# The scan's output and the gate rows ahead of the out projection: half of the output worked out inside the scan, gates broadcast by DMA

## The reference

```python
mu = jnp.mean(y, axis=-1, keepdims=True)
var = jnp.mean(jnp.square(y - mu), axis=-1, keepdims=True)
yn = ((y - mu) * lax.rsqrt(var + GN_EPS)).reshape(bn, s, A_WIDTH) * prm['gn_w'] + prm['gn_b']
bonus = jnp.sum(f['r'][:, :, None] * f['k'] * prm['r_k'], axis=(2, 4))
yn = yn + (bonus[..., None] * f['v']).reshape(bn, s, A_WIDTH)
return (yn * f['g']).astype(dtype)
...
return out_lat, jnp.concatenate([a_ctx, b_ctx], axis=-1) @ w_out
...
h_lat = h_lat + ml[2] * rms_norm_2(o_lat, g_post_mix[i])
```

## Time and profile before

| | |
|---|---|
| median of 3 runs | 2166.06 us |
| lowest, highest | 2158.6, 2166.61 us |
| the profiled execution | 2172.52 us |
| its span | 2169.9 us |
| granted clock, mean | 0.946 |
| busy share: PE, DVE, ACT, GpSimd | 91%, 53%, 41%, 12% |

### The profile page before, as it was taken

One profiled execution on the slowest core, in us unless ns is written; L12 is line 12 of the kernel. 1 busy time (PEld: TensorE's weight loads), 2 busy tenths in 40 slices (PEclk: granted clock), 3 DMA queues, 4 the chain that ended last, 5 costly groups with the idle time before them and its releaser, 6 DMA issues. The chain is left out here.

```text
span 2169.9 us, 36714 instructions
## 1 busy us (share of the span) xinstructions
PE 1977.5 (91%) x15607; PEld 1634.5 (75%) x15607; DVE 1142.5 (53%) x1799; ACT 880.5 (41%) x1560; POOL 257.0 (12%) x292
## 2 busy tenths in 40 slices
PE   5997999898899999997899968989999979888998
PEld 4746998675799788664788837878888768667986
DVE  4555675555577554346655574354444545435643
ACT  4354654445366443353322233232222344545542
POOL 1100221110022100003211071020000021002000
PEclk9987999998899999997899989999999989998999
...
GB/s 245 175 284 104 182 188 185 146 195 290 99 192 179 172 118 86 131 180 12 6 4 3 4 78 78 97 79 97 97 97 97 79 39 135 21 20 131 181 187 122
DMA packets 230936, 261.34 MB, mean 120 GB/s; under 512 B 14070, under 2 KB 153590, under 8 KB 230647
## 3 DMA queue, kind: packets, MB, share of 16 engines
...
q10 hardware_dynamic: 9424, 2.95, 0.7%
...
## 5 line engine op out<-in xcount | busy, mean ns | idle before, releaser
L399 PE MATMUL acc<-rounded,rounded 128*128 128x512 f32 (+1 forms) x2552 | 881.9, 346 | 35.7 <-DVE rounded L643 11.2
L400 PE MATMUL acc<-rounded,rounded 128*128 128x512 f32 (+1 forms) x2552 | 876.9, 344 | 0.0
L401 PE MATMUL acc<-rounded,rounded 128*128 128x512 f32 (+1 forms) x2552 | 875.9, 343 | 0.0
L383 DVE TENSOR_TENSOR rounded<-arena,rounded 128x2048 fp32r<-128x2048 f32 x194 | 435.3, 2248 | 321.2 <-ACT rounded L372 321.1
L399 PEld LDWEIGHTS acc<-rounded,rounded 128*128 128x128 f32 x2552 | 489.3, 192 | 103.4 <-issue 27.6
L401 PEld LDWEIGHTS acc<-rounded,rounded 128*128 128x128 f32 x2552 | 488.8, 192 | 61.0
L400 PEld LDWEIGHTS acc<-rounded,rounded 128*128 128x128 f32 x2552 | 489.3, 192 | 60.1 <-issue 0.5
L372 ACT ACTIVATE rounded<-arena 128x2048 fp32r<-128x2048 f32 x194 | 362.8, 1873 | 366.5 <-PE acc L401 330.5
L1901 PE MATMUL sc<-arena 64*64 64x64 f32 x2560 | 99.0, 226 | 13.6 <-DVE arena L2023 12.0
L1901 PEld LDWEIGHTS sc<-arena 64*64 64x64 f32 x2560 | 87.4, 139 | 23.4 <-DVE arena L2023 15.4
L1382 DVE SCALAR_TENSOR_TENSOR arena<-acc,pcol,arena 128x254 f32<-128x254 f32 (+1 forms) x176 | 76.8, 478 | 52.2 <-ACT arena L1363 50.6
...
## 6 DMA issues: line engine op xcount, KB each, us to landing
arena<-in_w_ff SPq DMA_DIRECT2D x64, 1024.0 KB, 5.3
arena<-in_w_ada SPq DMA_DIRECT2D x48, 1024.0 KB, 5.2
...
arena<-in_w_in SPq DMA_DIRECT2D x24, 1024.0 KB, 5.1
arena<-in_w_down SPq DMA_DIRECT2D x20, 1024.0 KB, 5.1
arena<-in_w_out SPq DMA_DIRECT2D x16, 1024.0 KB, 5.2
arena<-in_w_in_even SPq DMA_DIRECT2D x9, 1024.0 KB, 5.3
arena<-in_w_in_odd SPq DMA_DIRECT2D x8, 1024.0 KB, 5.2
```

The lines of the kernel that those rows point to most:

```text
L383: dve.tensor_tensor(r32(w), w, r32(high_slot(c)[:, 0:size(c)]), ALU.subtract).then_inc(split_made, 1)
L399: pe.matmul(ps, ah, bh, start=first, stop=False)
L400: pe.matmul(ps, ah, bl, start=False, stop=False)
L401: return pe.matmul(ps, al, bh, start=False, stop=last)
```

## The change

The head norm, turn, bonus and gate of the context half (tokens 0 to 255) are done in steps 4 to 7 of the scan: normed on DVE in steps 4 and 5 with the power on GpSimd, turned by PE in step 6 and combined by pairs of row tiles in steps 6 and 7. The bonus's additions and multiplications go from DVE to GpSimd, with `a_r_k` folded into a matrix once. The norm's gain and bias are applied as ACT copies the turned values. The low part of the result is made by GpSimd. The first chunk of `out2_0` is loaded during the scan and is the one with rows 4 to 7 (`PIECES`); the latent half's turn and products stand in PE's program before the first tiles of the second chunk. The gates are stored by six DMAs to a scratch in DRAM and read back into all partitions, one DMA per sublayer; diagonals, ones products and copies go. `tok_gemm` and `plan_tok` take the chunks of a block in the order `pieces`. Left out below are these two, the helpers' plans for banks of mix1 and ff1, and constructors.

```diff
--- before
+++ after
@@ -282,9 +283,10 @@
         f0 += len(tts)
-        for k0 in range(0, kts, 4):
+        order = pieces or range(0, kts, 4)
+        for k0 in order:
             chunks.append(view[:, k0:min(k0 + 4, kts), 512 * c:min(512 * c + 512, n)])
-            if k0 + 4 >= kts:
+            if k0 == order[-1]:
                 release.append((acc_full, f0))
@@ -455,11 +457,16 @@
     stage(("step", s), acc=12, tr=4, sc=4 * (LEVELS - 1))
-stage("gate_mix0", acc=4)
-stage("rwkv_out", acc=8, tr=8)
-stage("gate_ff0", acc=4)
+    if s == NCH - 2:
+        stage(("rwkv_turned", 0), tr=2)
+    if s >= NCH - 2:
+        stage(("rwkv_in", 0, s - (NCH - 2)), sc=2)
+stage(("rwkv_turned", 1), tr=2)
+for jp in range(2):
+    stage(("rwkv_in", 1, jp), sc=2)
 stage("post_mix0", acc=8)
-plan_tok("out2_0", I["w_out_2"][0], KT, acc_at["post_mix0"], [ALL] * 2)
+PIECES = (4, 0)
+plan_tok("out2_0", I["w_out_2"][0], KT, acc_at["post_mix0"], [ALL] * 2, PIECES)
 plan_norm(("ff", 0, 1))
@@ -681,13 +687,13 @@
                     before(b, k0, n)
-                ps = claim(pe, "acc", f + n) if k0 == 0 else bank("acc", f + n)
+                ps = claim(pe, "acc", f + n) if k0 == order[0] else bank("acc", f + n)
                 for k in range(kn):
                     ins = mm3(pe, ps[:, 0:width], lhsT(k0 + k, tt), both(w, lambda v: v[:, k, :]),
-                              k0 + k == 0, k0 + k == kts - 1)
-                if k0 + kn == kts:
+                              k0 == order[0] and k == 0, k0 == order[-1] and k == kn - 1)
+                if k0 == order[-1]:
                     ins.then_inc(acc_full, 1)
-            if k0 + kn < kts:
+            if k0 != order[-1]:
                 ins.then_inc(chunk_read, 1)
@@ -1890,6 +1893,16 @@
             step_identity(pool, d, s + 1)
+    if s == 3:
+        for j in range(4):
+            ins = pool.tensor_scalar(rk_ones[:, j, :], head_ones, col("a_r_k_2", j), None, ALU.mult)
+        ins.then_inc(rk_ones_set, 1)
+    if s == 4:
+        bonus_pool(pool, 0)
+    if s == 5:
+        gn_pool(pool, 0)
+    if s == NCH - 1:
+        bonus_pool(pool, 1)
@@ -1957,6 +1970,10 @@
         ins.then_inc(acc_full, 1)
+    if s == NCH - 2:
+        y_turned_pe(pe, 0)
+    if s >= NCH - 2:
+        rwkv_in_pe(pe, 0, s - (NCH - 2))
     for d, q in enumerate(scans):
@@ -2003,6 +2020,10 @@
                            ACT.Copy).then_inc(drain("acc", f), 1)
+        if what == "g" and s == NCH - 2:
+            y_affine_act(act, 0)
+    if s >= NCH - 2:
+        y_high_act(act, 0, s - (NCH - 2))
@@ -2038,6 +2059,12 @@
+    if s == 4:
+        gn_center_dve(dve, 0)
+    if s == 5:
+        gn_var_dve(dve, 0)
+    if s >= NCH - 2:
+        y_out_dve(dve, 0, s - (NCH - 2))
     for d, q in enumerate(scans):
@@ -2060,16 +2087,63 @@
         ins.then_inc(drain("acc", f), 1)
+    if s == 5:
+        gn_scale_dve(dve, 0)
...
+rk_ones = pA[:, 13, :].rearrange("p (j c) -> p j c", j=4)
+def stream_cols(x, hf, j0=0, j1=4):
+    return x[:, j0:j1, hf * SEQ:(hf + 1) * SEQ]
+def gn_of(x, hf):
+    return x[:, :].rearrange("p (j c) -> p j c", j=4)[:, :, 4 * hf:4 * hf + 4]
+def in_chunks(x, hf):
+    return stream_cols(x, hf).rearrange("p j (c v) -> p j c v", c=4)
+def gn_wide(x, hf):
+    return gn_of(x, hf).unsqueeze(3).broadcast_to([P, 4, 4, CH])
+def gn_center_dve(dve, hf):
+    for s in ((2, 3) if hf == 0 else (NCH - 2, NCH - 1)):
+        for d in range(2):
+            wait_drained(dve, "acc", chain_fill(s, d, "y"))
+    y, squares = y_st[:, :, 4 * hf:4 * hf + 4, :], in_chunks(lc[0], hf)
+    link(dve, dve.tensor_reduce(gn_of(gn_sum, hf), y, AX_X, ALU.add))
+    link(dve, dve.tensor_scalar(gn_of(gn_mean, hf), gn_of(gn_sum, hf), 1.0 / HD, None, ALU.mult))
+    link(dve, dve.tensor_tensor(y, y, gn_wide(gn_mean, hf), ALU.subtract))
+    link(dve, dve.tensor_tensor(squares, y, y, ALU.mult))
+def gn_var_dve(dve, hf):
+    link(dve, dve.tensor_reduce(gn_of(gn_sq, hf), in_chunks(lc[0], hf), AX_X, ALU.add))
+    dve.tensor_scalar(gn_of(gn_var, hf), gn_of(gn_sq, hf), 1.0 / HD, GN_EPS, ALU.mult, ALU.add).then_inc(gn_var_ready, 1)
+def gn_pool(pool, hf):
+    pool.wait_ge(gn_var_ready, hf + 1)
+    pool.tensor_tensor(gn_of(gn_rs, hf), gn_of(gn_var, hf), half[:, 0:16].rearrange("p (j c) -> p j c", j=4), ALU.pow).then_inc(gn_rstd, 1)
+def gn_scale_dve(dve, hf):
+    dve.wait_ge(gn_rstd, hf + 1)
+    y = y_st[:, :, 4 * hf:4 * hf + 4, :]
+    dve.tensor_tensor(y, y, gn_wide(gn_rs, hf), ALU.mult).then_inc(y_normed, 1)
+def bonus_pool(pool, hf):
+    x = stream_cols(kd[0], hf)
+    pool.wait_ge(bk_done[0], 2 * (4 if hf == 0 else NCH))
+    pool.wait_ge(bk_done[1], 2 * (4 if hf == 0 else NCH))
+    pool.tensor_tensor(x, x, stream_cols(kd[1], hf), ALU.add).then_inc(kd_summed, 1)
+    pool.wait_ge(kd_summed, hf + 1)
+    pool.tensor_tensor(x, x, stream_cols(rr, hf), ALU.mult).then_inc(bonus_in, 1)
@@ -2077,72 +2151,106 @@
+def rwkv_fill(hf, jp, i):
+    return sc_at[("rwkv_in", hf, jp)] + i
+def y_turned_pe(pe, hf):
+    pe.wait_ge(y_normed, hf + 1)
+    for jp in range(2):
+        ps = claim(pe, "tr", tr_at[("rwkv_turned", hf)] + jp)
+        for i in range(2):
+            for c in range(4):
+                for h in HEADS:
+                    at = (4 * i + c) * CH
+                    ins = pe.matmul(ps[h, at:at + CH], y_st[h, 2 * jp + i, 4 * hf + c, :], eye64[h, :], start=True, stop=True)
+        ins.then_inc(tr_full, 1)
+def rwkv_in_pe(pe, hf, jp):
+    if jp == 0:
+        pe.wait_ge(rk_ones_set, 1)
+        pe.wait_ge(bonus_in, hf + 1)
+        pe.wait_ge(g2_landed, 16)
+        pe.wait_ge(lora_in, 2)
+    bonus = claim(pe, "sc", rwkv_fill(hf, jp, 0))
+    for i in range(2):
+        j = 2 * jp + i
+        ins = pe.matmul(bonus[:, i * SEQ:(i + 1) * SEQ], rk_ones[:, j, :], kd[0][:, j, hf * SEQ:(hf + 1) * SEQ], start=True, stop=True)
+    ins.then_inc(sc_full, 1)
+    gate = claim(pe, "sc", rwkv_fill(hf, jp, 1))
+    for i in range(2):
+        j = 2 * jp + i
+        ins = pe.matmul(gate[:, i * SEQ:(i + 1) * SEQ], g2[:, j * P:(j + 1) * P], pA[:, 14, hf * SEQ:(hf + 1) * SEQ], start=True, stop=True)
+    ins.then_inc(sc_full, 1)
+def y_affine_act(act, hf):
+    for jp in range(2):
+        f = tr_at[("rwkv_turned", hf)] + jp
+        ps = filled(act, "tr", f)
+        for i in range(2):
+            j = 2 * jp + i
+            ins = act.activation(y_full[:, j, hf * SEQ:(hf + 1) * SEQ], ps[:, i * SEQ:(i + 1) * SEQ], ACT.Identity,
+                                 scale=col("a_gn_w_2", j), bias=col("a_gn_b_2", j))
+        ins.then_inc(drain("tr", f), 1)
+def y_out_dve(dve, hf, jp):
+    pair = lambda ps: ps[:, :].rearrange("p (j t) -> p j t", j=2)
+    cut = lambda x: stream_cols(x, hf, 2 * jp, 2 * jp + 2)
+    f, y, x = rwkv_fill(hf, jp, 0), cut(y_full), cut(lc[0])
+    dve.tensor_tensor(x, pair(filled(dve, "sc", f)), cut(vf), ALU.mult).then_inc(drain("sc", f), 1)
+    wait_drained(dve, "sc", f)
+    wait_drained(dve, "tr", tr_at[("rwkv_turned", hf)] + jp)
+    link(dve, dve.tensor_tensor(y, y, x, ALU.add))
+    dve.tensor_tensor(y, y, pair(filled(dve, "sc", f + 1)), ALU.mult).then_inc(drain("sc", f + 1), 1)
+def y_high_act(act, hf, jp):
+    wait_drained(act, "sc", rwkv_fill(hf, jp, 1))
+    act.activation(r32(stream_cols(yT[0], hf, 2 * jp, 2 * jp + 2)), stream_cols(y_full, hf, 2 * jp, 2 * jp + 2), ACT.Copy).then_inc(yA_high, 1)
+def y_low_pool(pool, hf, jp):
+    pool.wait_ge(yA_high, 2 * hf + jp + 1)
+    hi, lo = (stream_cols(v, hf, 2 * jp, 2 * jp + 2) for v in (yT[0], y_full))
+    pool.tensor_tensor(r32(lo), lo, r32(hi), ALU.subtract).then_inc(yA_low, 1)
 def rwkv_out_dve(dve):
...
+    ahead_dve(dve, chunk_at["out2_0"])
+    gn_center_dve(dve, 1)
+    gn_var_dve(dve, 1)
+    ahead_dve(dve, chunk_at["out2_0"] + 1)
+    gn_scale_dve(dve, 1)
+    for jp in range(2):
+        y_out_dve(dve, 1, jp)
     ahead_dve(dve, chunk_at["out2_0"] + HIGH - 1)
...
 def rwkv_out_act(act):
...
+    ahead_act(act, chunk_at["out2_0"])
+    ahead_act(act, chunk_at["out2_0"] + 1)
+    y_affine_act(act, 1)
+    for jp in range(2):
+        y_high_act(act, 1, jp)
+    ahead_act(act, chunk_at["out2_0"] + HIGH - 1)
+def out2_0_pe(pe):
+    def among(block, k0, n):
+        if (block, k0, n) == (0, 0, 0):
+            pe.wait_ge(yA_low, 2)
+            y_turned_pe(pe, 1)
+            rwkv_in_pe(pe, 1, 0)
+        if (block, k0, n) == (0, 0, 1):
+            rwkv_in_pe(pe, 1, 1)
+        if (block, k0, n) == (0, 0, 2):
+            pe.wait_ge(yA_low, 4)
+    for tt in (2, 3):
+        wait_drained(pe, "tr", tr_at["yTB"] + tt)
+    tok_gemm(pe, "out2_0", mix0.f0, KT, [ALL] * 2, mix_lhs(yT), before=among, pieces=PIECES)
@@ -2150,43 +2258,34 @@
...
-    def pool_gate(self, pool):
-        pool.wait_ge(mod_ready, 2 * DEPTH)
-        self.free(pool)
+    def gate_out(self, sp):
         for i, s in enumerate(self.streams):
+            sp.dma_start(gate_rows[self.rows_before + i].rearrange("(k p) -> p k", p=P),
```

(107 more changed lines are left out.)

71 lines of the change are left out of this document (10 added, 61 removed).

## The result

The changed kernel takes 2146.66 us, median of 4 runs (2145.6 to 2151.01), against 2166.34 before: ratio 0.9911, 95% interval 0.9885 to 0.9937. It is faster by 0.9%, inside the range of the prediction and 8.8 us above its forecast of 2137.9. The profiled execution is 2151.01 us (span 2149.2), against a span of 2169.9 before: 20.7 less where 28.2 were forecast.

What follows compares the result with a forecast made beforehand. Engines queued behind each other between scan and out2_0 were taken to bound the 91%-busy TensorE; 32.8 gained there, less 8.8 in the scan, plus 4.2 from gates, gave 28.2 less: 2137.9 us, range 2126 to 2153.

Steps and rivals of the forecast that it cites:

- The unknown: six small stores: SP's 6 x 1024 single-float stores ahead of the first chunk: 10 us per engine, 215 us of cover, cost 0.
- if a step under 4 grows: Sign of being wrong, in the scan: steps 0 to 4 were to last 27 us.
- Rival C: SP's queue ahead of out2_0: stores delay the first chunk, slower from 0.66 us an element, 2230 at 0.8; chance 0.02.
- 26 ns a packet: Price for the lone-float stores, from queue q10's 9424 small packets: 384 stores per engine are 10 us.
- Rival A: Scan steps 4 and 6 serialize: scan cost near 20, 11 us more, 2149 us; chance 0.13.
- B: In out2_0 the latent half comes late: PE stands 8 us or more, second cold start 1.8, 2147; chance 0.11.
- Start, product and stall: out2_0 behind the scan: start 4.5, cold clock 1.8, product 44.8, turns and products 5.8, stall 1.4; end S+58.3.
- slack of 3.7 us: Latent half under out2_0's first quarter: scaling ends at S+13.8, 3.7 us before PE asks, so hidden.
- The scan, 8.8 forecast: Context-half work added to steps 4 to 7 costs 0.2, 0.7, 5.7 and 2.2, sum 8.8; bounds 5.8 and 20.
- Gates elsewhere, 4.2 forecast: Gate products leaving mix1 and ff1 gain 2.5 and 1.7, sum 4.2 us; bounds 0 and 4.8.
- D: out2_0's chunk order still waits for the latent half: gain only 11.5, 2154.6 us; chance 0.04.

Runs made afterwards that it cites:

- whole-row kernel: Changed kernel with gates turned on TensorE and each row stored as 8 runs of 512 B, 48 packets for 6144: 2138.58 and 2138.39 us.
- doubled stores: Changed kernel with each gate row stored twice, to two scratches, so 12288 single floats: 2172.0 us.
- chunk behind the scan: Changed kernel with the first chunk of out2_0 loaded only behind the scan, as before: 2151.4 us.
- both halves behind the scan: whole-row kernel with the context half's norm, turn and products moved behind the scan too: 2146.7 us.
- whole rows spread: Changed kernel with six stores one behind each of steps 0 to 5, each row in 8 runs of 512 bytes: 2139.9 us.
- bonus later: whole-row kernel with GpSimd's latent-half bonus waiting for the first level of step 7: 2137.2 us.

## Why the prediction was right, and where it failed

The time lies in the range, and the mechanism behind the gap of out2_0 was right. One term failed.

**The failed step is "The unknown: six small stores"**, the line "I take 0". The packets were priced for one victim alone, the first chunk's landing 215 us later, and that part held. But lone floats also stall the engines of the scan while they are written: step 0 is 13.3 us longer than before, 13.7 longer than with whole rows, and 36.6 when doubled. The prediction's own sign of being wrong, "if a step under 4 grows", came. The profile before showed that instructions share the DMA engines, four packets of q8 in 22 us of scan, and I had not read that queue. Rival C, too, asked only how late the chunk would be; the missing rival was "the scan stands still while the stores are written". The 26 ns a packet taken from q10 fits neither case: the 1040 packets of a single store took 11.9% of 16 engines over 4 us, 7 ns of engine time each, six stores in a row (chunk behind the scan, 1030 to 1054 us) 109.4% over 24 us for 6238, 67 ns each. Neither price tells what a store cost the scan, 2 to 3 us. That the time still fell into the range is luck in part: the range's upper end was set for rivals A and B, and neither came.

**Start, product and stall.** First product S+4.9 (forecast 4.5). The clock was 0.51 for 2.98 us, which loses 1.5 (1.8); the 5.8 for the turns and products and the 44.8 for the product leave 0.2 unexplained; the stall was 0.6 (1.4). End S+57.8 (58.3). GpSimd's power of 16 columns took 4.88 us, not 2.9, and the slack of 3.7 us took it up; its low part took 1.28, not 1.80. The 2.9 was right by itself: the same power takes 2.94 in step 5. Behind the scan it starts at 1285.58, while DVE's low part runs:

```profile
1210.55 2.94 POOL L2132 TENSOR_TENSOR stat<-stat,half 128x16 f32<-128x16 f32 x1
...
1285.41 2.28 DVE L385 TENSOR_TENSOR rounded<-arena,rounded 128x2048 fp32r<-128x2048 f32 x1
```

DVE has 2.1 us left then, and the power takes 2.0 more. In the kernel with both halves behind the scan the first power stands beside the same instruction (2.1 us left, 4.91) and the second beside none (2.91). The prediction put the second low part beside the power and priced each as if it ran alone.

**The scan, 8.8 forecast.** Whole-row kernel against both halves behind: 7.5. By steps 4 to 7: 0.9, 0.5, 3.4 to 4.4, 2.0, against 0.2, 0.7, 5.7, 2.2. ACT's four copies, priced at 1.6 in step 6, seem hidden; DVE's centring in step 4 fits its hole less well than its rows said. Rival A's 20 did not come.

**Gates elsewhere, 4.2 forecast with bounds 0 to 4.8.** The 7.1 to 7.2 above come of single profiles and can't be held against this. What follows out2_0 took 823.0 us in the one profile of before, and 815.2 to 822.3 in the thirteen profiles of kernels whose gates come by DMA. The largest part of that spread stands between the last update of ff0 and that of mix1: 205.3 to 206.3 us in ten of the thirteen, with PE busy for 181, and 209.2 to 209.3 in three (doubled stores, chunk behind the scan, whole rows spread), with PE busy for 185 at a lower clock (0.78 in place of 0.94 in one stretch of 25 us). The profile before has 211.5, with PE busy for 186, 3.1 of it in the gate products, and doesn't tell which of the two it belongs to. So 2.2 to 6.2 us went there, beside the 2.5 forecast, and 0.8 to 2.2 in what follows (197.8 before, 195.6 to 197.0), beside the 1.7. How much of the 7.2 is the clock's stays open.

**Rivals B and D** did not come: no second cold start, and the first quarter did not wait.

The balance with the missing term: 28.2 - 13.3 = 14.9; steps 4 to 7 gave back 3.2, the gates 3.0 and out2_0's end 0.4, the start cost 0.9: 20.6, against 20.7 measured. That it closes says only that no stretch was left out: the 3.2 holds some 2 us in which the clock of the profile before was lower, and the 3.0 may hold as much. The whole-row kernel, without the missing term, has medians of 2138.6 and 2138.4 beside the forecast of 2137.9, and is the fastest here beside its like with the bonus later.
